# Delta-rule front of a hybrid decoder layer: another order of exponentials, bonus input and spare products

## The chip, the core and the metric

The kernel runs on one core of a Trainium2 chip. Its time is the device time in microseconds of one execution. All data are float32. The engines run their own programs side by side and meet at semaphores: TensorE (PE, with its weight loads PEld), VectorE (DVE), ScalarE (ACT), GpSimd (POOL), and SyncE (SP), whose queue issues most of the DMAs.

## The reference

Two identical layers act on 512 prompt tokens and 8 x 4 sample tokens (544 columns in the kernel). Each layer projects x to z (3592 columns), runs four mixers on groups of z, and then does an output projection, cross attention and an MLP. The change lies in the start of the fourth mixer, RWKV-7 with a delta rule:

```python
zs = z + (zprev - z) * mu                      # token shift
r, k, v, zw, za, zg = split(zs)
logw = -softplus(-(w0 + tanh(zw) @ w2)) - 0.5
decay = exp(-exp(logw))
a = sigmoid(a0 + za @ a2)
g = sigmoid(zg) @ g2
kk = k * k_k;  kk = kk / max(sqrt(sum(kk * kk)), 1e-12)
k = k * (1.0 + (a - 1.0) * k_a)
S = S * w - (S @ kk) outer (kk * a) + v outer k   # for each token
o = S @ r
bonus = sum(r * k * r_k) * v
```

## The kernel before, in words

Features lie on partitions and the 544 tokens on the free axis. z(f) is the tile of 128 features number f; T28 is z(28) and z(29), T30 is z(30) and z(31). X1, X2, X4 and X5 are scratch tiles of 2 x 544. A product by TensorE is split in two halves, of 256 and 288 columns. The first half of a product with bank number b goes to PSUM bank b, the second to bank b + 2. Each bank has a count of fillings and a count of releases, so that TensorE waits for the eviction of a bank's last content before it fills the bank again.

The projection takes w_in in slabs of 512 columns (four z tiles each), which DMAs bring into a ring with two slots. `gemm(n)` multiplies slab n, 16 products a z tile (8 of each half). The z tiles of slabs 4 to 6, and the keys and values of the memory behind them, are the list SPARE: `spare_products(pe, point, units, banks)` issues so many of its products at a place where TensorE would wait, and `spare_tiles(point)` on ScalarE evicts the halves that are complete by then. A profile shows each such product as two matmul instructions.

The order is written out by hand. On TensorE (from line 763): the products "kk" (sums of squares), tile 2 of slab 3, the wait for act_d, the products "wa" (four, two halves each) and "g2" (two, two halves each), tile 3 of slab 3, 16 spare products in banks 0 and 1 (FILL_BONUS), the wait for rk, the product "bonus", and a transpose for an output. Then the loop over five token tiles T starts: it waits for dfeat, transposes X2, X4, z(22) and z(24) ("dtok"), issues 2 spare products, waits for GpSimd's padded copies dpad, and forms the first scores ("dsc", line 815). The rest of the stage is TensorE work mixed with spare products.

On ScalarE (from line 1656): the evictions of tiles 0 to 2 of slab 3, tanh and sigmoid (act_d), the evictions of wa (sigmoid) and g2 (copy), Ln and Exp on kks (rn), the eviction of tile 3, and then, after the wait for S, three exponentials (expd 1 to 3), of X2, of X1 into T28 and of X1. The compiler puts a table load ahead of a function that the resident set lacks; `preload_act_table_set` names a set.

On VectorE (from line 1265): a scan over T28 into X1 and a subtraction into X2 (S), the wait for expd 3, two small copies into epc (the decays that the state updates read), the products of kk, the exponentials and a into X2 and X4, then X5 and rk, then r and k times their exponentials (dfeat). GpSimd copies X2 and r into padded tiles after dfeat.

Of the kernel before, what the change touches and what calls it, by code (L numbers as in the profile page):

```python
# [6 lines left out]
ALU = mybir.AluOpType  # L7
# [5 lines left out]
KC = D // P  # L13
DEPTH = 2
SEQ = 512
# [23 lines left out]
LN_EXP = "natural_log_exp_and_others"  # L39
# [6 lines left out]
ZR_D, ZK_D, ZV_D, ZWA_D, ZG_D = 20, 22, 24, 26, 27  # L46
# [173 lines left out]
def build(nc, A, O, table, where):  # L220

    with ExitStack() as ctx:
# [34 lines left out]
        def z(f, n=1):  # L257
            v = big[:, f * NT:(f + n) * NT]
            return v if n == 1 else v.rearrange("p (n t) -> p n t", n=n)
# [89 lines left out]
        sig = Signals(nc, ctx, "")  # L349
        bk = Banks(sig, psum)  # L350
        for l in range(DEPTH):
# [107 lines left out]
            omka = cols(tmp, region("tmp", 2), 2)  # L459
            mcar = cols(tmp, region("tmp", 4), 4)  # L460
            carry = cols(tmp, region("tmp", 24), 2, 12)
            epc = cols(tmp, region("tmp", 32), 2, 16)
            SsT = cols(tmp, region("tmp", 1024), 2, NB, HD)

            X1 = cols(tmp, region("tmp", 2 * NT), 2, NT)
            X2 = cols(tmp, region("tmp", 2 * NT), 2, NT)
# [60 lines left out]
            def segs(v):  # L527

                if len(v.shape) == 2:
                    return v[:, SEQ:].rearrange("p (b t) -> p b t", b=NB)  # L530
                return v[:, :, SEQ:].rearrange("p n (b t) -> p n b t", b=NB)
# [7 lines left out]
            def prm(name, i):  # L539
                return pc[:, ROWS[name][0] + i:ROWS[name][0] + i + 1]  # L540
# [70 lines left out]
            SPARE += [(n, None, nt, k) for n in range(7, 11) for nt in range(2) for k in range(KC)]  # L611
            HALF_DONE = {}

            FILL_BONUS = 2 * KC
            FILL_OM, FILL_X, FILL_ST, FILL_SA = 2, 2, 2, 1
            FILL_4 = 4
            FILL_D = (4, 16, 8)
# [3 lines left out]
            def spare_products(pe, point, units, banks, upto=None):  # L621

                at = HALF_DONE.get("at", 0)
                while at < len(SPARE) and (units > 0 if upto is None else at < upto):
                    n, f, half, k = SPARE[at]
                    key = ("kv", n - 7, half) if f is None else ("z", f, half)
                    if k == 0:
                        if half == 0 and (f is None or f == SLABS_IN[n][1]):
                            slab_pe(pe, n)
                        bk.begin(pe, key, banks[half])  # L630
                    bank = psum[:, bk.turn[key][0], :]
                    if f is None:
                        ins = pe.matmul(bank, memT[:, k, half * P:(half + 1) * P], wring[:, n % 2, k, :], start=(k == 0), stop=(k == KC - 1))  # L633
                    else:
                        c, i = HALVES[half][1], f - SLABS_IN[n][1]
                        ins = pe.matmul(bank[:, :c.stop - c.start], wring[:, n % 2, k, i * P:(i + 1) * P], xTv[:, k, c],  # L636
                                        start=(k == 0), stop=(k == KC - 1))
                    if k == KC - 1:
                        bk.filled(ins, key)
                    units -= 2 if f is None else 1  # L640
                    at += 1
                HALF_DONE["at"] = at
                HALF_DONE[point] = at // KC
# [77 lines left out]
            with nc.Block() as block:  # L721

                @block.tensor
                def _(pe):
                    def gemm(n, tiles=range(4)):
                        c0, f0 = SLABS_IN[n]
                        w = slab_pe(pe, n)
                        for i in tiles:
                            x_product(pe, ("z", f0 + i), (f0 + i) % 2, [w[:, k, i * P:(i + 1) * P] for k in range(KC)])
# [37 lines left out]
                    for i in range(2):  # L767
                        product(pe, ("kk", i), i, lambda k: kks[:, i, :], [const("sum64")])
                    gemm(3, (2,))
                    pe.wait_ge(sig["act_d"], sig.at("act_d", 2))  # L770
                    for i in range(4):
                        product(pe, ("wa", i), i % 2, lambda k: z(26)[:, :], [wwa[:, i, :]])
# [382 lines left out]
                def _(v):  # L1155
                    def one(ins):

                        after(v, ins, "v")
# [108 lines left out]
                        ins = v.tensor_tensor_scan(X1[:, i, :], const("keep_d"), T28[:, i, :], 0.0, ALU.mult, ALU.add)  # L1267
                    one(ins)
                    sig.up(tt(X2, X1, T28, ALU.subtract), "S")
                    v.wait_ge(sig["expd"], sig.at("expd", 3))  # L1270
                    v.tensor_copy(epc[:, :, 0:8], T28[:, :, 63:SEQ:64])
                    v.tensor_copy(epc[:, :, 8:16], segs(T28)[:, :, :, 3])
                    v.wait_ge(sig["rn"], sig.at("rn", 1))
                    one(tt(X4, kkr, kks, ALU.mult))
                    tt(X2, X4, X2, ALU.mult)
                    bk.given(v, ("wa", 3, 0))
                    bk.given(v, ("wa", 3, 1))
                    one(tt(X4, X4, T30, ALU.mult))
                    tt(X4, X4, X1, ALU.mult)
                    for i in range(2):  # L1280
                        ins = ts(T30[:, i, :], T30[:, i, :], prm("rwkv_k_a", i), omka[:, i:i + 1], ALU.mult, ALU.add)
                    one(ins)
                    one(tt(z(ZK_D, 2), z(ZK_D, 2), T30, ALU.mult))
                    for i in range(2):
                        ins = stt(X5[:, i, :], z(ZR_D + i), prm("rwkv_r_k", i), z(ZK_D + i), ALU.mult, ALU.mult)
                    sig.up(ins, "rk")
                    v.wait_ge(sig["rk"], sig.at("rk", 1))
                    tt(z(ZR_D, 2), z(ZR_D, 2), T28, ALU.mult)
                    sig.up(tt(z(ZK_D, 2), z(ZK_D, 2), X1, ALU.mult), "dfeat")
# [289 lines left out]
                def _(s):  # L1579
# [7 lines left out]
                    def z_tiles(n, tiles=range(4)):  # L1587

                        for i in tiles:
                            for half, c in HALVES:  # L1590
                                z_half(SLABS_IN[n][1] + i, half, c)
# [19 lines left out]
                    def spare_tiles(point):  # L1611

                        while spare_read[0] < HALF_DONE[point]:
                            n, f, half, _ = SPARE[KC * spare_read[0]]
                            if f is None:
                                kv_half(n, half)
                            else:
                                z_half(f, half, HALVES[half][1])
                            spare_read[0] += 1
# [37 lines left out]
                    s.wait_ge(sig["zs"], sig.at("zs", 2))  # L1657
                    sig.up(act(z(26)[0:64, :], z(26)[0:64, :], ACT.Tanh), "act_d")
                    sig.up(act(z(27), z(27), ACT.Sigmoid), "act_d")
                    for i in range(4):  # L1660
                        both(("wa", i), z(28 + i), ACT.Sigmoid, bias=prm(("rwkv_w0", "rwkv_a0")[i // 2], i % 2))
                    for i in range(2):
                        both(("g2", i), z(26 + i), ACT.Copy)

                    s.wait_ge(sig["ss"], sig.at("ss", 1))
                    after(s, act(kks, kks, ACT.Ln, scale=1048576.0), "s")
                    sig.up(act(kks, kks, ACT.Exp, scale=-0.5, bias=const("eps")[:, 2:3]), "rn")
                    z_tiles(3, (3,))
                    s.wait_ge(sig["S"], sig.at("S", 1))
                    sig.up(act(X2, X2, ACT.Exp, scale=-RW_C), "expd")  # L1670
                    sig.up(act(T28, X1, ACT.Exp, scale=-RW_C), "expd")
                    s.wait_ge(sig["expd"], sig.at("expd", 2))
                    sig.up(act(X1, X1, ACT.Exp, scale=RW_C), "expd")
                    spare_tiles("bonus")

                    for T in range(5):
# [1156 lines left out]
```

## Time and profile before

| quantity | value |
|---|---|
| median of 3 runs | 2476.25 us (2476.14 to 2477.13) |
| the profiled execution | 2476.93 us, of it the span 2475.0 us |
| TensorE matmul busy | 2363.3 us, 95% |
| VectorE, ScalarE busy | 41%, 19% |
| mean granted TensorE clock | 0.972 |

The time lies 1.93 us above the span. The front that the change touches runs once in each layer: from 155 to 193 us of the span, and again 1219 us later. A timeline lists instructions in order of start, merged where they follow each other; a number in brackets is the idle time of the engine before them, with what ended it.

### The profile page before, as it was taken

To read this page: it belongs to the slowest core of one execution; us is meant where nothing else is said; L and a number is where in the kernel's file an instruction comes from. 1 tells how busy PE (TensorE), PEld (TensorE's weight loads), DVE (VectorE), ACT (ScalarE), POOL (GpSimd) and SP (SyncE) were. 2 spreads that over 40 slices of the span, in tenths; PEclk is the share of its full clock that TensorE was granted. 3 is DMA by queue.
4 is the path that set the end of the run, shared out by engine and by line. 5 is a ranking of instruction groups with operands and counts; after the bars stand their busy time and mean duration, and the time that the engine had idled before them with its cause. 6 is when DMAs were issued, how large, how long until landed. Compare 5 with 4: busy or idle time off the path is not lost. (4 is left out here: it accounts for less than half of the span.)

```text
span 2475.0 us, 31491 instructions
## 1 busy us (share of the span) xinstructions
PE 2363.3 (95%) x13278; PEld 1725.5 (70%) x13278; DVE 1009.3 (41%) x1851; ACT 458.6 (19%) x965; POOL 111.1 (4%) x208
## 2 busy tenths in 40 slices
PE   7989998979999999999999899989799999999997
PEld 5867774544884788888887677655458748888886
DVE  3243224553043644566132422436331336446742
ACT  2341122010130222100023321220111312220000
POOL 0001100100000000000001011001000000000000
PEclk9999999979999999999999999989799999999998
DMA  7110003143342222232231111023432341132220
GB/s 266 42 68 19 19 35 91 47 130 120 138 171 103 85 100 71 71 100 68 68 122 68 35 37 35 24 72 98 162 136 102 120 151 54 68 102 68 90 81 36
DMA packets 137675, 215.04 MB, mean 87 GB/s; under 512 B 35528, under 2 KB 69632, under 8 KB 137408
## 3 DMA queue, kind: packets, MB, share of 16 engines
q1 hardware_dynamic: 135232, 208.84, 24.8%
q10 hardware_dynamic: 2304, 4.20, 0.5%
q8 instruction: 106, 1.74, 0.3%
q14 instruction: 33, 0.27, 0.0%
HBM read 198.43 MB, written 14.58 MB: 86 GB/s over the span
## 5 line engine op out<-in xcount | busy, mean ns | idle before, releaser
L589 PE MATMUL psum<-xT,ring 128*128 128x256 f32 (+1 forms) x1536 | 358.4, 395 | 3.2 <-ACT xT L320 1.6
L589 PEld LDWEIGHTS psum<-xT,ring 128*128 128x128 f32 x1536 | 292.3, 191 | 64.7 <-issue 3.2
L636 PE MATMUL psum<-xT,ring 128*128 128x256 f32 (+1 forms) x768 | 221.9, 415 | 0.1
L2100 PE MATMUL psum<-tmp 128*128 128x272 f32 x768 | 181.4, 393 | 0.0
L2100 PEld LDWEIGHTS psum<-tmp 128*128 128x128 f32 x768 | 145.8, 190 | 30.8 <-issue 0.8
L636 PEld LDWEIGHTS psum<-xT,ring 128*128 128x128 f32 x768 | 133.6, 191 | 41.0 <-issue 15.2
L633 PE MATMUL psum<-ring,ext 128*128 128x512 f32 x256 | 121.5, 616 | 4.5 <-ACT ext L1604 4.5
L2201 PE MATMUL psum<-big,ring 128*128 128x256 f32 (+1 forms) x512 | 118.5, 393 | 0.4 <-DMA ring<-in_w_down 0.3
L2511 PE MATMUL psum<-ring,big 128*128 128x512 f32 x256 | 113.1, 595 | 0.0
L2010 PE MATMUL psum<-ring,big 128*128 128x512 f32 x256 | 111.6, 594 | 0.0
L2201 PEld LDWEIGHTS psum<-big,ring 128*128 128x128 f32 x512 | 97.0, 190 | 20.7 <-DMA ring<-in_w_down 1.0
L2100 PE MATMUL psum<-xT,ring 128*128 128x272 f32 x448 | 107.2, 392 | 0.0
L1597 ACT ACTIVATE big<-psum 128x256 f32<-128x256 f32 (+1 forms) x112 | 44.4, 396 | 312.1 <-PE psum L589 191.9
L2100 PEld LDWEIGHTS psum<-xT,ring 128*128 128x128 f32 x448 | 85.0, 190 | 17.4
L2151 PE MATMUL psum<-big,ring 128*128 128x272 f32 x384 | 91.6, 392 | 0.0
L633 PEld LDWEIGHTS psum<-ring,ext 128*128 128x128 f32 x256 | 48.7, 199 | 60.4 <-issue 56.1
L2010 PEld LDWEIGHTS psum<-ring,big 128*128 128x128 f32 x256 | 48.0, 190 | 60.8 <-issue 60.8
L2511 PEld LDWEIGHTS psum<-ring,big 128*128 128x128 f32 x256 | 47.4, 190 | 56.9 <-issue 56.9
L2046 DVE SCALAR_TENSOR_TENSOR xtok<-xtok,psum 128x512 f32<-128x512 f32 (+1 forms) x40 | 27.3, 682 | 140.1 <-PE psum L2010 86.5
L2151 PEld LDWEIGHTS psum<-big,ring 128*128 128x128 f32 x384 | 72.6, 190 | 14.7
L2151 PE MATMUL psum<-xT,tmp 128*128 128x272 f32 x288 | 68.6, 392 | 0.0
L2151 PE MATMUL psum<-tmp 128*128 128x272 f32 x288 | 68.0, 392 | 0.0
(476 smaller groups left out, 3281.6 us busy)
## 6 DMA issues: line engine op xcount, KB each, us to landing
ring<-in_w_down SPq DMA_DIRECT2D x16, 2048.0 KB, 8.1
ring<-in_w_in SPq DMA_DIRECT2D x14, 2048.0 KB, 8.3
ring<-in_w_up SPq DMA_DIRECT2D x14, 2048.0 KB, 7.7
big<-in_cache_mem_k SPq DMA_DIRECT2D x16, 1024.0 KB, 5.0
ring<-in_xa_wk SPq DMA_DIRECT2D x4, 2048.0 KB, 7.9
ring<-in_xa_wv SPq DMA_DIRECT2D x4, 2048.0 KB, 10.3
ring<-in_w_out SPq DMA_DIRECT2D x4, 2048.0 KB, 9.3
tmp<-in_cache_mem_v SPq DMA_DIRECT2D x8, 1024.0 KB, 10.0
```

The source lines that it names most:

```text
L589: ins = pe.matmul(ps[:m, :w], lhsT_list[k], rhs(k)[:, c], start=(k == 0), stop=(k == n - 1))
L633: ins = pe.matmul(bank, memT[:, k, half * P:(half + 1) * P], wring[:, n % 2, k, :], start=(k == 0), stop=(k == KC - 1))
L636: ins = pe.matmul(bank[:, :c.stop - c.start], wring[:, n % 2, k, i * P:(i + 1) * P], xTv[:, k, c], start=(k == 0), stop=(k == KC - 1))
L1597: bk.give(act(z(f)[:, c], ps[:, 0:c.stop - c.start], fn, scale=scale), ("z", f, half))
L2010: ins = pe.matmul(ps[:n, :], left[k][:, t0:t0 + n], w[half][:, k, :], start=(k == 0), stop=(k == KC - 1))
L2046: bk.give(v.scalar_tensor_tensor(x, x, ALPHA, ps[:n, :], ALU.mult, ALU.add), key)
L2100: ins = pe.matmul(ps[:, :HT], left[:, k, :], right[:, k, :], start=(k == 0), stop=(k == KH - 1))
L2151: ins = pe.matmul(ps, left[:, k, :], right[:, k, :], start=(g == 0 and k == 0), stop=(g == 3 and k == KH - 1))
L2201: ins = pe.matmul(ps, w[r][:, k, i * P:(i + 1) * P], hT[:, 2 * KC * r + k, c], start=(r == half and k == 0), stop=(r != half and k == 2 * ...
L2511: ins = pe.matmul(ps, aT[:, k, t0:t0 + n], w[:, k, :], start=(k == 0), stop=(k == KC - 1))
```

## The change

The exponentials of the front move ahead of the eviction of z tile 3, with one named table set loaded ahead of the Ln. VectorE makes the bonus input (rk) right after S. The factor made from k_a goes to X5 instead of over T30, and a in T30 stays as it is for the product into X4. The single wait for expd 3 becomes one for expd 1 and one for expd 3 further on. Of the 16 spare products ahead of the bonus, 8 (the first half of z tile 4) move ahead of the wait for act_d, into bank 3, with their eviction ahead of those of wa. The other 8 stay, in bank 1.

```diff
-            FILL_BONUS = 2 * KC
+            FILL_BONUS = KC
@@ tensor
                     gemm(3, (2,))
+                    spare_products(pe, "wa", KC, (3, 0))
                     pe.wait_ge(sig["act_d"], sig.at("act_d", 2))
@@ vector
                     sig.up(tt(X2, X1, T28, ALU.subtract), "S")
-                    v.wait_ge(sig["expd"], sig.at("expd", 3))
-                    v.tensor_copy(epc[:, :, 0:8], T28[:, :, 63:SEQ:64])
-                    v.tensor_copy(epc[:, :, 8:16], segs(T28)[:, :, :, 3])
-                    v.wait_ge(sig["rn"], sig.at("rn", 1))
-                    one(tt(X4, kkr, kks, ALU.mult))
-                    tt(X2, X4, X2, ALU.mult)
                     bk.given(v, ("wa", 3, 0))
                     bk.given(v, ("wa", 3, 1))
-                    one(tt(X4, X4, T30, ALU.mult))
-                    tt(X4, X4, X1, ALU.mult)
                     for i in range(2):
-                        ins = ts(T30[:, i, :], T30[:, i, :], prm("rwkv_k_a", i), omka[:, i:i + 1], ALU.mult, ALU.add)
+                        ins = ts(X5[:, i, :], T30[:, i, :], prm("rwkv_k_a", i), omka[:, i:i + 1], ALU.mult, ALU.add)
                     one(ins)
-                    one(tt(z(ZK_D, 2), z(ZK_D, 2), T30, ALU.mult))
+                    one(tt(z(ZK_D, 2), z(ZK_D, 2), X5, ALU.mult))
                     for i in range(2):
                         ins = stt(X5[:, i, :], z(ZR_D + i), prm("rwkv_r_k", i), z(ZK_D + i), ALU.mult, ALU.mult)
                     sig.up(ins, "rk")
+                    v.wait_ge(sig["rn"], sig.at("rn", 1))
+                    one(tt(X4, kkr, kks, ALU.mult))
+                    v.wait_ge(sig["expd"], sig.at("expd", 1))
+                    one(tt(X2, X4, X2, ALU.mult))
+                    one(tt(X4, X4, T30, ALU.mult))
+                    v.wait_ge(sig["expd"], sig.at("expd", 3))
+                    tt(X4, X4, X1, ALU.mult)
+                    v.tensor_copy(epc[:, :, 0:8], T28[:, :, 63:SEQ:64])
+                    v.tensor_copy(epc[:, :, 8:16], segs(T28)[:, :, :, 3])
@@ scalar
                     sig.up(act(z(27), z(27), ACT.Sigmoid), "act_d")
+                    spare_tiles("wa")
...
+                    s.preload_act_table_set(LN_EXP)
                     s.wait_ge(sig["ss"], sig.at("ss", 1))
                     after(s, act(kks, kks, ACT.Ln, scale=1048576.0), "s")
                     sig.up(act(kks, kks, ACT.Exp, scale=-0.5, bias=const("eps")[:, 2:3]), "rn")
-                    z_tiles(3, (3,))
                     s.wait_ge(sig["S"], sig.at("S", 1))
                     sig.up(act(X2, X2, ACT.Exp, scale=-RW_C), "expd")
                     sig.up(act(T28, X1, ACT.Exp, scale=-RW_C), "expd")
                     s.wait_ge(sig["expd"], sig.at("expd", 2))
                     sig.up(act(X1, X1, ACT.Exp, scale=RW_C), "expd")
+                    z_tiles(3, (3,))
                     spare_tiles("bonus")
```

## Rows read from the trace of the kernel before

**Rows 1.** The page, part 1: busy time, share of the span, instructions of TensorE.

```profile
PE 2363.3 (95%) x13278; PEld 1725.5 (70%) x13278; DVE 1009.3 (41%) x1851; ACT 458.6 (19%) x965; POOL 111.1 (4%) x208
```

**Rows 2.** The waits of TensorE, whole span: total, times, longest.

```profile
PE psum L589 <- DVE tmp L1285: 10.9, 2, 5.5
...
PE psum L589 <- ACT big L1659: 6.0, 2, 3.0
...
PE psum L2201 <- DMA ring<-in_w_down: 0.3, 1, 0.3
```

**Rows 3.** Timeline of TensorE, layer 0: start, length, line, shapes, count, idle before.

```profile
147.81 7.50 PE L589 MATMUL psum<-xT,ring 128*128 128x256 f32 x32
158.31 7.45 PE L589 MATMUL psum<-big,tmp 128*128 128x256 f32 x24 [3.01 <-ACT big L1659]
166.20 7.57 PE L589 MATMUL psum<-xT,ring 128*128 128x256 f32 x32 [0.43 <-ACT big L1624]
...
186.54 4.00 PE L589 MATMUL psum<-tmp,con 128*128 128x256 f32 x8 [5.44 <-DVE tmp L1285]
...
190.54 1.06 PE L802 MATMUL psum<-con,tmp 128*128 128x128 f32 x4
...
193.34 1.08 PE L815 MATMUL psum<-xtok,tmp 128*64 128x256 f32 x8
```

**Rows 4.** Windows: length, busy time of each engine, granted clock, DMA.

```profile
158.31:166.20 7.89, 7.46 (x25) 5.64 (x25) 3.27 (x3) 5.20 (x12) 0.00 (x0) 0.78 0.00 0
166.20:181.10 14.90, 14.90 (x64) 12.04 (x64) 4.18 (x6) 9.25 (x11) 0.00 (x0) 1.00 0.42 140
186.54:193.34 6.80, 6.80 (x21) 5.37 (x22) 4.45 (x7) 1.20 (x2) 1.59 (x4) 0.56 0.01 2
```

**Rows 5.** Timeline of ScalarE, same stretch.

```profile
162.19 2.58 ACT L1624 ACTIVATE big<-psum,tmp 128x288 f32<-128x288 f32 x5 [0.31 <-PE psum L589]
164.81 1.69 ACT L1624 ACTIVATE big<-psum 128x256 f32<-128x256 f32 x4
166.51 1.28 ACT L1666 ACT_TABLE_LOAD   x1
...
168.93 1.28 ACT L1667 ACT_TABLE_LOAD   x1
...
176.24 1.11 ACT L1673 ACTIVATE tmp<-tmp 128x1088 f32<-128x1088 f32 x1
```

**Rows 6.** Timeline of VectorE, same stretch.

```profile
162.90 2.48 DVE L1267 TENSOR_TENSOR_SCAN tmp<-con,big 128x544 f32<-128x544 f32 x2 [10.99 <-ACT big L1624]
...
177.56 1.29 DVE L1274 TENSOR_TENSOR tmp<-xtok 128x1088 f32<-128x1088 f32 x1
...
182.62 1.03 DVE L1281 TENSOR_SCALAR big<-big,tmp 128x544 f32<-128x544 f32 x2
183.68 1.29 DVE L1283 TENSOR_TENSOR big<-big 128x1088 f32<-128x1088 f32 x1
185.01 1.48 DVE L1285 SCALAR_TENSOR_TENSOR tmp<-big,tmp 128x544 f32<-128x544 f32 x2
...
187.73 1.28 DVE L1289 TENSOR_TENSOR big<-big,tmp 128x1088 f32<-128x1088 f32 x1
```

**Rows 7.** Timeline of GpSimd, same stretch.

```profile
190.56 0.40 POOL L1810 COPY xtok<-big 64x256 f32<-64x256 f32 x1
```

**Rows 8.** Timeline of TensorE at the second token tile.

```profile
269.42 0.66 PE L802 MATMUL psum<-con,tmp 128*128 128x128 f32 x4
...
271.30 1.08 PE L815 MATMUL psum<-xtok,tmp 128*64 128x256 f32 x8
```

**Rows 9.** Timeline of ScalarE, end of the stage: a named set loaded ahead.

```profile
403.15 1.28 ACT L1746 ACT_TABLE_LOAD   x1 [0.47 <-ACT ext L1604]
...
416.23 1.11 ACT L1743 ACTIVATE big<-big 128x1088 f32<-128x1088 f32 x1
```

**Rows 10.** DMA view, 124 to 134 us, 40 slices of 0.25 us: rate of each.

```profile
GB/s 41 16 57 164 262 360 401 385 336 319 344 377 410 418 410 410 418 393 401 385 401 426 401 385 246 123 82 16 0 0 0 0 0 0 0 0 0 0 0 0
```

## The prediction

> **What bounds the kernel now.** I read four views, in this order. The page's first part: TensorE is busy for 95% of the span [rows 1]. All its work stays, so only its idle time and its slowed time can be won or lost. The waits of TensorE come next. In the whole span only a few stand out, and two lie in the front: for the act_d sigmoid, 6.0 us over the two layers, and for the bonus input, 10.9 us over the two layers [rows 2]. Then the timelines of the front of layer 0. TensorE idles 3.01 us ahead of wa, 0.43 ahead of z tile 3, and 5.44 ahead of the bonus [rows 3]. Last the windows, for the clock. After the idle 3.01 us the granted clock is 0.78 on average up to 166.20, after 5.44 it is 0.56 up to 193.34, and between them, with the gap of 0.43 just before, it is 1.00 [rows 4]. These are mixtures of the two levels, 1.2 and 2.4 GHz. So each long gap costs its own length and then slow work behind it. In layer 1 the same waits come back with the same lengths, so I work out layer 0 and double it.
>
> **What a layer can give back.** The idle time is 3.01 + 0.43 + 5.44 = 8.9 us. The slow work: the 24 instructions of wa and g2 take 7.5 us, and a z tile's 32 take 7.50 at the full clock [rows 3], 0.234 each, so they would take 5.6: 1.8 lost. The 8 of the bonus and a transpose take 4.00 from 186.54 to 190.54, where 9 would take 2.0: 2.0 lost. From the first dtok transpose to the first dsc product the same work takes 2.80 here [rows 3] and 1.88 at the next token tile [rows 8]: 0.9 lost. Together 13.6 us a layer. Now I lay out the changed order to see what it keeps of that.
>
> **The first half of z tile 4 moved ahead of act_d.** TensorE comes there at 155.31 (147.81 + 7.50). Eight products of 256 columns are 256/544 of a tile, 3.5 us, 3.6 with the tail: to 158.9. It fills the gap that ends at 158.31, so wa begins 0.6 later than before, but at the full clock. Two waits come with it. The slab must be in the ring: its transfer runs from about 124 to 131 us [rows 10], more than 24 us early. Bank 3 must be free: its last user, the second half of kk, came before tile 2 of slab 3, which itself took 7.5 us. Behind the new eviction on ScalarE stand the wa evictions, but it starts at 158.9, takes what the 256-column evictions of g2 take (1.69 for four, 0.42 each [rows 5]), and the first wa product is only full at 159.4. It is free. Its cover is TensorE's own first wa product of 0.5 us; without it the 0.4 would be on the path. SP's queue sees the same order: slab 5 waits for tile 3 of slab 3, and its issue moves with that. If some 13 us of other work behind it vanish, it still has the rest of slab 4 in front of it, 56 products, over 25 us of TensorE.
>
> **wa, g2 and S.** At the full clock ScalarE limits this piece: five wa evictions in 2.58 us, 0.52 each [rows 5]. Four are done by 161.5, eight by 163.6, g2 at 165.3. VectorE's scan waited for the fourth and began at 162.90 [rows 6]. Now it begins at 161.7, and with 2.48 for the scans and 1.29 for the subtraction S is there at 165.5. TensorE finishes g2 at about 164.5 and waits for bank 1: tile 3 began 1.39 after the first g2 eviction (164.81 to 166.20), so now at 165.0. That is 0.5 idle, like the 0.43 before, which was followed by a clock of 1.00. Tile 3 ends at 172.4.
>
> **The bonus input made without the exponentials.** After S VectorE does only the k_a step (1.03), the product (1.29) and the r_k step (1.48): from 182.62 to 186.5 in the old order, 3.9 us. So rk comes at 169.4 instead of 186.5. TensorE is then in tile 3 and the 5.44 us wait is gone with 7 us to spare. What is late next is ScalarE and dfeat.
>
> **The table and the exponentials.** Before, Ln and Exp each have a load of 1.28 [rows 5]. The named set at the end of the stage serves a Ln and then an Exp with no load between them; one load stands at 403.15 and the Exp at 416.23 is reached without another [rows 9]. So one load remains: from 165.3 the load to 166.6, Ln to 167.8, Exp to 169.0 (rn, before at 171.4). S is long there, and three exponentials of 1.11 (less a little overlap) end at 172.1 instead of 177.35.
>
> A page sees the table otherwise. The Trainium skill, ScalarE: Activation LUTs, section "What ACT_TABLE_LOAD costs", gives 1283 ns for the load and about 1380 ns more for a drain, 2.66 us a switch. The trace shows the 1.28, with Ln starting within 0.03 us of the load's end. By the page's figure, an estimate, the exponentials would end 1.4 later and the forecast lose about 2.8 us over both layers; the row decides for me.
>
> **The eviction of z tile 3 behind them.** Both halves are late now, and bank 1 is wanted by the spare half that stays ahead of the bonus. The first half of tile 3 is evicted from 172.1 to 172.5, and TensorE is done with tile 3 at 172.4: idle 0.1. The second half follows at once. If the exponentials ended later, each microsecond would fall on TensorE: this is the tightest place of the new order. The spare half of 288 columns takes 3.9, to 176.4, and the bonus 1.9, to 178.3. A transpose of 0.1 follows, and dtok could begin at 178.4 instead of 190.54.
>
> **dfeat.** VectorE starts the kk product at 169.4 (rn at 169.0 is there). With a step of 1.32 (a product and the wait for its write) three products reach 173.4; expd 1 (170.0) and expd 3 (172.1) are there in time. The product with X1 (1.25), two copies (0.2) and the last two products (2.5) give dfeat at 177.3, instead of 189.0 [rows 6]. GpSimd then takes its four copies, which ended at 190.96, 1.95 after dfeat [rows 7]: at 179.3. TensorE begins dtok at 178.4 and reaches dsc at 180.3. Both are 1.0 us ahead of need. In VectorE's queue the bonus evictions stand behind dfeat and end at 178.8, before dsc wants it. The two copies into epc cost 0.2 and are hidden by that 1.0; the added waits for writes cost 0.04 each.
>
> **The sum.** dsc at 180.3 instead of 193.34 is 13.05 us: the 13.6 to be had less 0.55 of new idle time. Two layers give 26.1. All waits of TensorE behind it hang on work that moves along; only one transfer row lies behind the front, 0.3 us [rows 2]. So the profiled execution's 2476.93 becomes 2450.8; it lies 0.7 above the median, so the median becomes 2450.2.
>
> **The rivals.**
> *The clock does not come back* (0.12). The gap of 0.5 at 164.5, or one left in a place I misjudge, still lets it fall once in the front. For it: it fell after each of the two long gaps. Against it: 1.00 after 0.43. One slow piece costs what one costs here, 1.8 to 2.9 a layer, so 2450.2 + 3.6 to 5.8: 2454 to 2456.
> *The table is not kept* (0.08). If each of Ln and Exp is still given its load, that part of the change does not do what it says: the exponentials end 1.3 later, 173.4, and the spare half starts 1.2 to 1.3 late. dfeat moves by less. It is 2.5 us over both layers, 2453, and with another load for the following exponentials and a slow piece up to 2461.
> *Hidden elsewhere* (0.04). If the next stage were held by something that does not move, a transfer above all, nothing would come: 2476. Against it speak the 0.3 us of TensorE's waits on w_down [rows 2].
> *Slower* (0.03). The moved half makes wa wait for slab 4. It decides once the slab lands more than 13 us after 155.3, at 168; a landing at 175 would give 7 us a layer of loss, 2490. The transfer is over at 131.
>
> **Chances and range.** The forecast's own case has 0.73, from 2447 to 2455. Its upper end has the page's drain, or a step of 1 to 2 us at the tight place in each layer; its lower end has all 13.6 and a slow piece less behind later gaps of the stage (about 1 us a layer). The two next cases reach to 2461. I give 2446 to 2460. About 0.2%, 5 us, is what a measurement of this kernel can tell from no change. Faster by more: 0.73 + 0.12 + 0.08 = 0.93; within: 0.04; slower: 0.03.
>
> **What would show it.** In the timeline of the changed kernel: 16 instructions of spare products in the old gap at 155.3; wa at 158.9 and tile 3 at 165.0; a clock of 1.00 from 155 to 181; one table load and rk at 169.4; tile 3's evictions after 172.1; bonus at 176.4 without idle time, dtok at 178.4, dsc at 180.3. The forecast is wrong if the spare half starts well after 172.5, if dfeat is later than 178.4, if a slow piece stands anywhere in the front, or if the waits behind 193 us grow.

## The result, and the profile after

| | before | changed |
|---|---|---|
| median in the runs side by side | 2476.25 us (5 runs) | 2452.03 us (5 runs, 2449.74 to 2452.35) |
| ratio of the times | | 0.99, 95% interval 0.9889 to 0.9912 |
| profiled execution, span | 2476.93, 2475.0 us | 2451.32, 2449.4 us |

The change makes the kernel 24.2 us faster. The forecast was 26.1, so 2450.2. The page of the changed kernel gives the span and the busy times (compare [rows 1]):

```profile
span 2449.4 us, 31491 instructions
...
PE 2356.6 (96%) x13278; PEld 1719.7 (70%) x13278; DVE 1009.8 (41%) x1851; ACT 455.5 (19%) x963; POOL 110.6 (5%) x208
```

TensorE's busy time is 6.7 us less for the same 13278 matmuls, because fewer of them ran at the lower clock. The waits of TensorE (total, times, longest) no longer hold the two of [rows 2]. The gap ahead of tile 3 is what is left of the front. The wait at L981 far behind the front stayed, and so did the small one for a transfer:

```profile
PE psum L981 <- DVE tmp L1409: 7.1, 2, 3.6
...
PE psum L589 <- ACT big L1626: 1.1, 2, 0.6
...
PE psum L2205 <- DMA ring<-in_w_down: 0.2, 1, 0.2
```

The timeline of TensorE through the front of layer 0, which answers to [rows 3], follows. Everything lies 1.42 us earlier from the start, since tile 2 begins at 146.39 instead of 147.81. The whole of it is there within the first 56 us, ahead of every changed instruction; 1.1 us of it is the wait for the kernel's first transfer, 16.7 us in the trace before and 15.6 in this one. So it is no part of the change, and I add it where I compare with the forecast's times.

```profile
146.39 7.50 PE L589 MATMUL psum<-xT,ring 128*128 128x256 f32 x32
153.72 3.62 PE L636 MATMUL psum<-xT,ring 128*128 128x256 f32 x16
157.18 5.66 PE L589 MATMUL psum<-big,tmp 128*128 128x256 f32 x24
163.39 7.57 PE L589 MATMUL psum<-xT,ring 128*128 128x256 f32 x32 [0.55 <-ACT big L1626]
170.81 4.15 PE L636 MATMUL psum<-xT,ring 128*128 128x288 f32 x16
174.80 2.00 PE L589 MATMUL psum<-tmp,con 128*128 128x256 f32 x8
...
176.75 0.60 PE L803 MATMUL psum<-con,tmp 128*128 128x128 f32 x4
...
178.58 1.08 PE L816 MATMUL psum<-xtok,tmp 128*64 128x256 f32 x8
```

Where two gaps of 3.01 and 5.44 us stood, one row follows the other. The spare half (153.72) fills the first. wa takes 5.66 instead of 7.45, the bonus 2.00 instead of 4.00, and the four dtok transposes 0.60 instead of 1.06. The timeline of ScalarE (compare [rows 5]):

```profile
157.38 0.38 ACT L1599 ACTIVATE big<-psum 128x256 f32<-128x256 f32 x1 [0.54 <-PE psum L636]
...
163.71 1.28 ACT L1668 ACT_TABLE_LOAD   x1
165.00 1.11 ACT L1670 ACTIVATE xtok<-xtok 128x1088 f32<-128x1088 f32 x1
...
169.38 1.11 ACT L1676 ACTIVATE tmp<-tmp 128x1088 f32<-128x1088 f32 x1
170.39 0.37 ACT L1599 ACTIVATE big<-psum 128x256 f32<-128x256 f32 x1
```

There is one table load, with Ln beginning at its end, and the exponentials end at 170.5, with tile 3's eviction behind them. VectorE (compare [rows 6]): the scan, the r_k step that gives rk at 167.6, the kk product that follows at once, and the last product that ends in dfeat at 175.4, 13.6 us earlier than before and 1.3 us before TensorE wants it.

```profile
160.09 2.48 DVE L1268 TENSOR_TENSOR_SCAN tmp<-con,big 128x544 f32<-128x544 f32 x2 [9.60 <-ACT big L1626]
...
166.20 1.48 DVE L1278 SCALAR_TENSOR_TENSOR tmp<-big,tmp 128x544 f32<-128x544 f32 x2
167.60 1.29 DVE L1281 TENSOR_TENSOR tmp<-xtok 128x1088 f32<-128x1088 f32 x1
...
174.15 1.28 DVE L1291 TENSOR_TENSOR big<-big,tmp 128x1088 f32<-128x1088 f32 x1
```

The windows (length, busy time of PE, PEld, DVE, ACT and POOL with counts, granted clock, DMA) show the clock at 1.00 throughout, where [rows 4] had 0.78 and 0.56:

```profile
155.30:159.00 3.70, 3.70 (x18) 3.17 (x17) 0.00 (x0) 3.00 (x6) 0.00 (x0) 1.00 0.00 0
159.00:165.00 6.00, 5.45 (x25) 4.29 (x24) 4.84 (x6) 5.68 (x11) 0.00 (x0) 1.00 0.00 0
165.00:172.50 7.50, 7.50 (x33) 5.91 (x32) 7.36 (x7) 6.11 (x7) 0.00 (x0) 1.00 0.06 7
172.50:178.00 5.50, 5.50 (x30) 4.57 (x29) 4.98 (x10) 1.03 (x3) 1.58 (x4) 1.00 1.00 360
```

### The profile page after: what moved, and what is told of

It reads as the page before. It is cut to its first block and busy times, and to the rows that moved or that the text cites. A ratio compares the mean times of both kernels' runs of the same rounds, so it can differ in the third digit from the quotient of the medians.

```text
span 2449.4 us, 31491 instructions
## 1 busy us (share of the span) xinstructions
PE 2356.6 (96%) x13278; PEld 1719.7 (70%) x13278; DVE 1009.8 (41%) x1851; ACT 455.5 (19%) x963; POOL 110.6 (5%) x208
## 5 line engine op out<-in xcount | busy, mean ns | idle before, releaser
L1599 ACT ACTIVATE big<-psum 128x256 f32<-128x256 f32 (+1 forms) x112 | 44.3, 396 | 312.6 <-PE psum L589 187.9
L2104 PEld LDWEIGHTS psum<-xT,ring 128*128 128x128 f32 x448 | 85.0, 190 | 17.4
```

Source lines behind the costliest of these rows:

```text
L1599: bk.give(act(z(f)[:, c], ps[:, 0:c.stop - c.start], fn, scale=scale), ("z", f, half))
L2104: ins = pe.matmul(ps[:, :HT], left[:, k, :], right[:, k, :], start=(k == 0), stop=(k == KH - 1))
```

## The experiments

To compare kernels I cut the span at four starts that each trace has: z tile 2 of slab 3, the first dsc product, the transposes of the sample states (L980 in the kernel before, some 240 us in), and the first product of the output projection. Front is the time from the first to the second, loop from the second to the third, rest from the third to the fourth, in us, layer 0 / layer 1. "Between" goes from the output projection of layer 0 to tile 2 of slab 3 in layer 1, "behind" from the output projection of layer 1 to the end of the span. These are differences of starts in the timelines, of one profiled execution a kernel; medians are those of the timed runs.

| kernel | median | front | loop | rest | between | behind |
|---|---|---|---|---|---|---|
| before | 2476.25 | 45.5 / 45.3 | 204.1 / 204.1 | 155.4 / 157.3 | 814.0 | 701.6 |
| changed | 2452.03 | 32.2 / 32.2 | 205.7 / 205.7 | 155.5 / 155.5 | 814.7 | 701.4 |
| e1_half_only | 2475.81 | 43.1 / 43.1 | 205.7 / 205.7 | 155.5 / 155.6 | 814.2 | 704.1 |
| e2_order_only | 2460.74 | 36.8 / 36.7 | 205.6 / 205.7 | 155.5 / 157.3 | 814.1 | 701.3 |
| e3_no_set | 2455.89 | 33.5 / 33.5 | 205.6 / 205.7 | 155.5 / 157.3 | 814.4 | 701.7 |
| e4_tile_first | 2455.56 | 34.9 / 34.9 | 207.2 / 204.2 | 155.5 / 155.4 | 814.7 | 703.9 |
| e5_input_late | 2465.09 | 39.8 / 39.3 | 205.7 / 205.8 | 155.5 / 155.6 | 811.7 | 703.9 |
| e6_no_set_bank0 | 2455.52 | 32.9 / 32.9 | 205.7 / 205.7 | 155.5 / 155.5 | 814.2 | 704.3 |
| e7_half_before_tile | 2447.92 | 31.3 / 31.3 | 207.2 / 204.2 | 155.6 / 155.5 | 811.5 | 704.1 |
| e8_more_fill | 2434.77 | 32.2 / 32.2 | 205.7 / 205.7 | 146.3 / 148.1 | 814.2 | 701.2 |
| e9_both | 2430.95 | 31.3 / 31.3 | 205.6 / 204.1 | 147.9 / 147.9 | 814.2 | 701.1 |
| e10_mixed_small | 2443.81 | 32.2 / 32.2 | 206.1 / 206.2 | 152.3 / 152.2 | 811.3 | 704.0 |
| e11_all | 2446.63 | 31.3 / 31.3 | 206.1 / 206.1 | 150.3 / 153.1 | 814.3 | 704.3 |
| e12_mixed_same | 2436.26 | 31.3 / 31.3 | 206.2 / 208.0 | 146.5 / 147.9 | 814.5 | 704.1 |

e8, e9, e11 and e12 have some 3.6 us of spare products in the loop where a wait was, and e10 and e11 have 3.4 us of them set among other matmuls of the loop. The kernel before, run beside these, had medians from 2475.01 to 2476.82.

**e1_half_only: the moved half alone.**

```diff
 (against the kernel before)
-            FILL_BONUS = 2 * KC
+            FILL_BONUS = KC
                     gemm(3, (2,))
+                    spare_products(pe, "wa", KC, (3, 0))
...
                     sig.up(act(z(27), z(27), ACT.Sigmoid), "act_d")
+                    spare_tiles("wa")
```

> The kernel before with only the spare half of z tile 4 moved ahead of act_d. My theory: the wait ahead of wa (3.0 us) goes and wa runs at the full clock, but TensorE has 8 spare products fewer ahead of the bonus and rk comes only some 1.2 us earlier, because it hangs on the three exponentials and the old order on VectorE. The wait ahead of the bonus grows from 5.4 to about 9 us. dtok gains 1.2 us a layer: 2474 us. Rival, parts that add up: the filled gap gives its 3.0 and 1.8 us in each layer by itself: 2466.5 us.

2475.81 us against 2475.01 of the kernel before beside it, ratio 1.0002 (0.9993 to 1.0012): no difference. TensorE in layer 0, as it ends the spare half, waits for the bonus, and begins dtok:

```profile
171.48 4.04 PE L636 MATMUL psum<-xT,ring 128*128 128x288 f32 x16
184.41 3.93 PE L589 MATMUL psum<-tmp,con 128*128 128x256 f32 x8 [8.89 <-DVE tmp L1286]
...
188.29 0.60 PE L803 MATMUL psum<-con,tmp 128*128 128x128 f32 x4
```

The wait for rk is 8.89 us, as expected. The wait ahead of wa went into it. The front is 2.2 to 2.5 us shorter, more than the 1.2 that I gave it, because the clock is back by dtok this time (0.60 for the four transposes). So filled by itself, the first gap mostly makes the second longer, and the parts do not add up: the fronts of both layers gain 4.6 us here, 17.4 in e2_order_only, and 26.4 together. Why nothing at all is left in the time, the trace shows in pieces that the edit does not touch: the loops are 1.6 us longer in each layer and the piece behind is 2.6 longer, against 1.7 less in the rest of layer 1.

**e2_order_only: the new order alone.**

```diff
 (against the changed kernel)
-            FILL_BONUS = KC
+            FILL_BONUS = 2 * KC
                     gemm(3, (2,))
-                    spare_products(pe, "wa", KC, (3, 0))
...
-                    spare_tiles("wa")
```

> The changed kernel with all 16 spare products back ahead of the bonus, so only the new order on ScalarE and VectorE and the single table load. My theory: the wait for rk (5.4 us) and the slow work behind it (2.9 us) go, the gap ahead of wa stays with its slow work: 8.3 us a layer, 2459.6 us. Rival, idle time alone counts and the clock does not: 10.9 us in all, 2465.4. If the parts added up, this gain and that of the half alone would make the whole 24.2 us; I expect them to make about 19.

2460.74 us (0.9939, 0.9924 to 0.9954). The gap ahead of wa and its slow work are there, and the bonus follows without any:

```profile
157.95 7.31 PE L589 MATMUL psum<-big,tmp 128*128 128x256 f32 x24 [3.01 <-ACT big L1660]
...
180.43 2.00 PE L589 MATMUL psum<-tmp,con 128*128 128x256 f32 x8
```

The front gained 8.8 and 8.6 us a layer, where 8.3 was expected and idle time alone would give 5.4. The clock's part is real. In the times the two halves of the change give 0 and some 14 us by themselves and 24 together.

**e3_no_set: the table load back.**

```diff
 (against the changed kernel)
-                    s.preload_act_table_set(LN_EXP)
```

> The changed kernel without the named table set, so that Ln and Exp have a load each again. My theory: the eviction of z tile 3 stands behind the exponentials and TensorE's spare half waits for its bank, so the 1.3 us of a load fall on TensorE in full: an idle 1.2 to 1.4 us ahead of the spare half in each layer, 2454.5 us, or up to 2 us more if the clock falls behind that gap. Rival: the exponentials have slack, nothing changes, 2452. By the drain that a page of the Trainium skill gives (ScalarE: Activation LUTs, What ACT_TABLE_LOAD costs) the load would cost 2.66 us, an estimate of 2457.

2455.89 us, 3.9 more than the changed kernel. TensorE waits ahead of the spare half, by the eviction of tile 3 (L1599):

```profile
172.73 4.15 PE L636 MATMUL psum<-xT,ring 128*128 128x288 f32 x16 [1.13 <-ACT big L1599]
```

The front is 1.3 us longer in each layer: one load of 1.28, in full, as forecast, and with no drain beside it: in this trace the second load begins 0.02 us after the end of the Ln, and the Exp 0.02 us after the load's. The Trainium skill's 2.66 us for a switch (ScalarE: Activation LUTs, What ACT_TABLE_LOAD costs) would have made it 2.7 us a layer, an estimate; the measurement is 1.3. The times show 1.3 us more than the two fronts; in the trace the rest of layer 1 is 1.8 us longer, 157.3 instead of 155.5, far from the change.

**e4_tile_first: tile 3 evicted ahead of the exponentials.**

```diff
 (against the changed kernel)
+                    z_tiles(3, (3,))
                     s.wait_ge(sig["S"], sig.at("S", 1))
...
                     sig.up(act(X1, X1, ACT.Exp, scale=RW_C), "expd")
-                    z_tiles(3, (3,))
```

> The changed kernel with z tile 3 evicted ahead of the exponentials again. My theory: the second half of the tile is only full at 172.4 in the forecast's frame, the exponentials end 4 us later, VectorE waits for the first of them at 170.8 until about 173.9, and dfeat comes at 180.4 instead of 177.3. TensorE waits about 2.1 us for dfeat ahead of dtok, in each layer, and the clock may fall behind that gap for another 1 to 2 us: 2456 to 2460 us. The bonus input is not touched and TensorE does not wait for it. Rival: dfeat has slack enough and nothing changes, 2452.

2455.56 us, 3.5 more. The wait is for dfeat (the last product of VectorE, L1291), ahead of dtok, and a second small one follows ahead of dsc:

```profile
177.70 0.66 PE L803 MATMUL psum<-con,tmp 128*128 128x128 f32 x4 [2.28 <-DVE big L1291]
...
179.89 1.08 PE L816 MATMUL psum<-xtok,tmp 128*64 128x256 f32 x8 [0.23 <-DVE tmp L1295]
```

The front is 2.7 us longer. The 2.28 agrees with the 2.1 forecast. The clock did not fall behind it inside the front (1.00 from 176 to 184 us). By the medians only 3.5 us are lost where two fronts make 5.4; the profiled execution was the slowest of the four, 6.1 us above that of the changed kernel. And the loops of the two layers differ by 3.0 us, 207.2 and 204.2, at the same program.

**e5_input_late: VectorE in the old order.**

```diff
 (against the changed kernel; the block up to rk as before)
+                    v.wait_ge(sig["expd"], sig.at("expd", 3))
+                    v.tensor_copy(epc[:, :, 0:8], T28[:, :, 63:SEQ:64])
+                    v.tensor_copy(epc[:, :, 8:16], segs(T28)[:, :, :, 3])
+                    v.wait_ge(sig["rn"], sig.at("rn", 1))
+                    one(tt(X4, kkr, kks, ALU.mult))
+                    tt(X2, X4, X2, ALU.mult)
...
```

> The changed kernel with VectorE's part in the old order: the wait for all three exponentials first, the bonus input last. My theory: rk comes 9.1 us after the third exponential (172.1 in the forecast's frame), at 181.2, and TensorE is ready for the bonus at 176.4: a wait of 4.8 us and some 3 us of slow work behind it in each layer, 7.7 us, so 2467 us. Rival, idle time alone: 2461.6. Rival, the early exponentials are what gives the gain and the order on VectorE nothing: 2452.

2465.09 us, 13.1 more. The bonus waits 4.72 us and runs slowly again, the front is 7.6 and 7.1 us longer:

```profile
177.98 3.99 PE L589 MATMUL psum<-tmp,con 128*128 128x256 f32 x8 [4.72 <-DVE tmp L1286]
```

**e6_no_set_bank0: no set, and the spare half in another bank.**

```diff
 (against the changed kernel)
-                    s.preload_act_table_set(LN_EXP)
...
-                    spare_products(pe, "bonus", FILL_BONUS, (0, 1))
+                    spare_products(pe, "bonus", FILL_BONUS, (0, 0))
```

> The changed kernel without the named table set, as in an earlier run, and with the second spare half in bank 0 instead of bank 1. Bank 0 is free once g2 is evicted, so the spare half no longer waits for the eviction of z tile 3. My theory (the table's price is paid through that bank): the 1.3 us a layer come back almost whole, because dfeat is then at 178.3 against TensorE's 178.4: 2452, at most 2453.5. Rival (the price is paid elsewhere, in rn and dfeat): it stays as slow as without the set in bank 1.

2455.52 us, so by the times my number was missed. In the trace the wait ahead of the spare half is gone, as it should be if the price is paid through bank 1. But the bonus's own first half goes into bank 0 as well and now waits for the eviction of the spare half, which I had overlooked:

```profile
176.35 2.08 PE L589 MATMUL psum<-tmp,con 128*128 128x256 f32 x8 [0.59 <-ACT big L1599]
```

The front is 0.7 us longer than changed instead of 1.3. The theory of the bank holds, the repair was only half of one. The two fronts make 1.4 of the 3.5 us by which the kernel is slower; the piece behind is 2.8 us longer, where the program is the same.

**e7_half_before_tile: the second half moved too.**

```diff
 (against the changed kernel)
-                    gemm(3, (3,))
-                    spare_products(pe, "bonus", FILL_BONUS, (0, 1))
+                    spare_products(pe, "bonus", FILL_BONUS, (0, 0))
+                    gemm(3, (3,))
...
-                    z_tiles(3, (3,))
                     spare_tiles("bonus")
+                    z_tiles(3, (3,))
```

> The changed kernel with the second spare half moved ahead of z tile 3, into bank 0, and its eviction ahead of that of tile 3. My theory: it fills the 0.55 us that TensorE waits for bank 1 behind g2 and removes the dependence on the exponentials; dtok comes 0.6 us earlier in each layer, 1.2 us in all, too little for the times to tell (2450.8 against 2452.0) but seen in the timeline: no idle time ahead of tile 3, dsc 0.55 earlier. Rival: dtok then waits for dfeat or dsc for the padded copies and nothing moves.

2447.92 us, 4.1 less than changed. The front is 0.9 us shorter in each layer (0.6 forecast) and has no gap:

```profile
156.03 5.66 PE L589 MATMUL psum<-big,tmp 128*128 128x256 f32 x24
161.53 4.04 PE L636 MATMUL psum<-xT,ring 128*128 128x288 f32 x16
165.41 7.50 PE L589 MATMUL psum<-xT,ring 128*128 128x256 f32 x32
```

The remaining 2.3 us are not the front's. In the trace the piece between the layers is 3.2 us shorter, the start 1.1, and the piece behind 2.6 longer.

**e8_more_fill: a gap elsewhere, filled the same way.**

```diff
 (against the changed kernel)
-                            spare_products(pe, ("Sss",), FILL_4, (0, 1))
+                            spare_products(pe, ("Sss",), FILL_4 + 8, (0, 1))
```

> The changed kernel with 8 more units (4 products of the memory's keys and values) at the wait for the sample states behind the delta rule, where TensorE still idles 3.6 us in each layer. My theory, that a gap of this length costs itself and slow work behind it: the 3.6 us and about 1.7 us of slow work go, and the products are missing later only where they stood in front of nothing: up to 5 us a layer, 2442. Rival: the slab of the third product is not there yet, or the units are missing at a later wait, and TensorE waits just as long there: 2452.

2434.77 us, 17.3 less than changed, where I had expected at most 10. Two gaps of the changed kernel in layer 0:

```profile
384.28 1.09 PE L981 MATMUL psum<-con,tmp 128*128 128x128 f32 x8 [3.56 <-DVE tmp L1409]
...
399.92 2.10 PE L589 MATMUL psum<-big,con 128*128 128x256 f32 x8 [2.21 <-ACT big L1742]
```

With the four added products (eight instructions) the row ahead of L981 ends as L981 begins, and the second gap is gone too:

```profile
379.51 5.42 PE L633 MATMUL psum<-ring,ext 128*128 128x512 f32 x12
385.07 1.09 PE L981 MATMUL psum<-con,tmp 128*128 128x128 f32 x8
```

The loop is as long as before, with products in place of the wait, and the rest is 9.2 and 7.4 us shorter: some 3.6 are those products, 2.2 the second gap, and the other 1.6 to 3.4 slow work. I had counted one gap only. The rest can be shorter by those products because they were only moved: they stand in the loop now.

**e9_both: both edits.** The diff is that of e7_half_before_tile and e8_more_fill.

> The two edits that were fastest by themselves together: the second spare half ahead of z tile 3, and 8 more units at the wait for the sample states. The stretches should add, since they lie 200 us apart: the front 31.3 us (0.9 less than changed) and the stretch behind the sample states 8 to 9 us less than changed. Changed 2452.0, the fill alone 2434.8, less 1.8: 2433 us, with 1 to 3 us either way for where the clock falls later. Rival, the clock's own pieces swallow it: 2435 to 2437.

2430.95 us, ratio 0.9819 to the kernel before (0.9805 to 0.9834), 21 us less than the changed kernel: the two add up, and of all versions run this is the fastest.

**e10_mixed_small: the clock inside the loop.** The changed kernel's windows of 2 us near the end of the loop of layer 0 (length, busy times, clock):

```profile
344.00:346.00 2.00, 2.00 (x60) 1.68 (x58) 1.45 (x3) 0.00 (x0) 0.00 (x0) 1.00 0.04 8
346.00:348.00 2.00, 2.00 (x59) 1.92 (x56) 0.00 (x0) 1.57 (x3) 0.00 (x0) 0.95 0.00 0
348.00:350.00 2.00, 2.00 (x28) 1.89 (x27) 0.00 (x0) 1.97 (x3) 0.00 (x0) 0.50 0.00 0
```

TensorE is busy without a break and its clock falls to 0.50 all the same, where the products that read the sample states stand, 128 matmuls of four columns in 64 rows each:

```profile
344.32 2.03 PE L922 MATMUL psum<-xtok,tmp 64*64 64x4 f32 x64
...
346.65 2.66 PE L931 MATMUL psum<-xtok,tmp 64*64 64x4 f32 x64
...
351.21 3.79 PE L636 MATMUL psum<-xT,ring 128*128 128x288 f32 x8
```

In the front 16 instructions of spare products of 288 columns take 4.15 us; here eight take 3.79. The same place in the kernel before:

```profile
361.39 2.13 PE L930 MATMUL psum<-xtok,tmp 64*64 64x4 f32 x64
...
365.43 2.68 PE L636 MATMUL psum<-xT,ring 128*128 128x288 f32 x8
```

There the clock falls as well, but a little later, and it is back after some 3.5 us; in the changed kernel it stays at 0.50 for some 7 us. From the start of the first 64 to the end of the eight instructions it is 9.0 us before and 10.7 in the changed kernel, with the same work. This is where the loop gave back 1.6 us a layer. The experiment sets spare products among them:

```diff
 (against the changed kernel, in the branch of the last token tile)
+                                if pr == 0:
+                                    spare_products(pe, ("KSmid", 0), 2, (0, 1))
                             bk.filled(ins, ("KS",))
+                            spare_products(pe, ("KSmid", 1), 2, (0, 1))
...
+                                if pr == 0:
+                                    spare_products(pe, ("KSmid", 2), 2, (0, 1))
                             sig.up(ins, "Dstates")
```

> The changed kernel with 6 more spare units set among the 128 matmuls of four columns that read the sample states at the last token tile (2 in the middle of the first 64, 2 behind them, 2 in the middle of the other 64). In the changed kernel the clock falls inside this run although TensorE has no idle time, and stays at half for some 7 us. Theory A, the clock falls because the four-column matmuls keep the array little busy: with full-sized products between them it stays at 1.00, which gives back 3 to 3.5 us a layer; the wait of 3.6 us behind may shrink too, as the 2.8 us of added products lie in front of it and are missing only in the rest behind: 2440 to 2446 us. Theory B, the fall comes from elsewhere (a fixed budget or a moment): the clock still falls there and only the wait behind may shrink: 2450 us.

2443.81 us, 8.2 less than changed, with one of the four runs at 2449.75. The second 64 matmuls now take 1.10 for each 32, the product between them is fast, and the clock is 1.00:

```profile
347.69 1.10 PE L934 MATMUL psum<-xtok,tmp 64*64 64x4 f32 x32
348.72 1.18 PE L636 MATMUL psum<-xT,ring 128*128 128x288 f32 x4
349.84 1.10 PE L934 MATMUL psum<-xtok,tmp 64*64 64x4 f32 x32
```

```profile
349.00:351.00 2.00, 2.00 (x37) 1.55 (x37) 0.00 (x0) 1.97 (x3) 0.00 (x0) 1.00 0.00 0
```

The three pieces of added products take 3.4 us, and the loop is only 0.4 longer, so 3.0 us shorter for the same work. The wait at the sample states did not shrink; it is 4.07 us. Loops and rests together are 5.6 us shorter in the two layers. The piece between them is 3.4 shorter and the piece behind 2.6 longer, neither of which the edit touches.

**e11_all: all three edits.** The diff is that of e9_both and e10_mixed_small.

> All three edits together: second spare half ahead of z tile 3, 8 more units at the sample states, 6 units among the four-column matmuls. If theory A of the mixed matmuls holds, 6 to 7 us less than the two edits without it: 2427 us; if the clock falls there anyway, 2433.

2446.63 us (2440.79 to 2451.33): a miss, 16 us slower than e9_both. The clock stays up in the loops as in e10. But of the 13.1 us that the span is longer than that of e9_both, 7.5 are in the rest of the two layers, 2.4 in the loops and 3.2 behind the rest of layer 1. In the rest a wait is new:

```profile
PE psum L1055 <- DVE xtok L1459: 3.4, 2, 1.7
```

In e9_both ten instructions of spare products, 4.46 us, stand at that place; here none is left. Within 2 us behind the wait the clock falls. In the rests of the two layers it is at half for some 45 and 52 us, in e9_both for 39 and 38. The piece behind is 704.3 instead of 701.1, which other kernels show too; the last section tells what differs in it.

**e12_mixed_same: the same number of units, four of them in other places.**

```diff
 (against e9_both)
+                                if pr == 0:
+                                    spare_products(pe, ("KSmid", 0), 2, (0, 1))
                             bk.filled(ins, ("KS",))
...
+                                if pr == 0:
+                                    spare_products(pe, ("KSmid", 2), 2, (0, 1))
                             sig.up(ins, "Dstates")
                             swap(0)
-                            spare_products(pe, ("KS",), FILL_4, (0, 1))
+                            spare_products(pe, ("KS",), 0, (0, 1))
```

> The kernel of the two fastest edits (second spare half ahead of z tile 3, 8 more units at the sample states; 2430.95 us) with the 4 units that stood behind the four-column matmuls of the last token tile moved among them, 2 into the middle of each 64. The number of spare products at every later place is the same, unlike in the runs with 6 more units. If the clock falls there because the four-column matmuls keep the array little busy, it now stays at 1.00 and 1.5 to 3.5 us a layer come back: 2424 to 2428 us. If 16 us of later stages suffered in the run of all three edits for another reason than the missing units, it is again near 2440. If the place of the products does not matter: 2431.

2436.26 us, 5.3 more than e9_both: a miss, and none of the three forecasts (2424 to 2428, 2431, 2440) fits. The loops are 4.5 us longer in the trace, the piece behind 3.0, the rest of layer 0 1.4 shorter. With 4 units instead of 6 the clock fell, and it fell earlier, so that a spare product itself ran slowly (2.14 us for four instructions instead of 1.24):

```profile
342.46 1.24 PE L636 MATMUL psum<-xT,ring 128*128 128x288 f32 x4
...
346.05 2.14 PE L636 MATMUL psum<-xT,ring 128*128 128x288 f32 x4
348.12 1.87 PE L933 MATMUL psum<-xtok,tmp 64*64 64x4 f32 x32
```

So spare products among the four-column ones kept the clock up with six units, in both layers, and did not with four. Whether their number decides, or the place of the missing two (between the two groups of 64), was not tried.

## Why the prediction was right

**The front.** Every step came as written. In the forecast's frame, with the shift of 1.42 added: wa at 158.6 (158.9 forecast), tile 3 at 164.8 (165.0), the scan at 161.5 (161.7), rk at 169.0 (169.4), the third exponential's end at 171.9 (172.1), the spare half at 172.2 (172.5), the bonus at 176.2 (176.4), dfeat at 176.9 (177.3), dtok at 178.2 (178.4), dsc at 180.0 (180.3). The gain is 13.3 and 13.1 us a layer where 13.05 was the sum. The differences all begin with wa's 0.3 us, and two readings share it. The spare half starts 7.33 us after tile 2, not 7.50, because rows that follow each other overlap a little and the forecast added the row's length. And it takes 3.46 us from its start to that of wa, not 3.6.

**What it is made of.** e2 shows the clock's share: 8.7 us of front for 5.4 us of gap. e1 shows that the moved half is worth 2.2 to 2.5 us of front while rk is late, and the whole change has 4.5 to 4.6 more of it than e2's order alone, e5 that the bonus input made early is worth 7.1 to 7.6 us a layer, e4 that the order of exponentials and tile eviction is worth 2.7, e3 that the table load is worth 1.3. e3 and e6 show that the last is paid at the eviction of tile 3, the place that the forecast called the tightest, with a step of 1.3 for a load of 1.28.

**The rivals.** The clock came back and stayed at 1.00 through the front, so the first rival fell there. The table was kept; the drain that the Trainium skill gives is not in the trace, and e3 prices the load without it. The slab was in the ring, and no transfer took the gain: the one transfer wait behind the front is 0.2 us.

**What was mis-sized.** 1.9 us between 26.1 and 24.2, 0.5 between the spans (25.6). The step "all waits of TensorE behind it hang on work that moves along" is right, but the slow pieces do not simply move along. The loop went from 204.1 to 205.7 us in each layer, 3.2 us given back, because the clock stays at half for some 7 us there instead of 3.5; the rest of layer 1 gained 1.8; the long piece between the layers went from 814.0 to 814.7; the start gave 1.4 that has nothing to do with the change. 26.4 - 3.2 + 1.8 - 0.8 + 1.4 is 25.6. So the fronts came by the mechanism that was forecast, and that the total lies so near is partly luck: the other pieces moved by 0.8 to 3.2 us and happened to cancel almost. In e1, e4, e5, e6 and e7 the piece behind is 2.3 to 2.7 us longer than in the kernel before, with the same program; here it kept its length. The forecast had allowed about 1 us a layer for a slow piece less, and nothing for one more, which is what came.

## What to carry to other kernels

Where the busiest engine waits at two places in a row, ask what the second wait hangs on before the first is filled: the filler alone gave nothing in the time (2.2 to 2.5 us a layer in the front), the earlier input alone 14 us, both 24. Price a long gap of TensorE with the slow work behind it: behind the gaps of 3.0 us and more it was half as much again, and filling two gaps of 5.8 us together gave 7 to 9 a layer. The shorter ones have no fixed price: 2.28 us in e4 was followed by no slow work in the front, 1.7 us in e11 was. And compare spans cut at the same instructions, for a change at one place can give or take a few microseconds at places that it does not touch.

## What the runs showed of the hardware

**The clock falls inside busy TensorE.** In every kernel but e10 and e11 the granted clock goes to 0.50 during or just behind 128 matmuls of four columns, in both layers, with no idle time in the rows. It stays there for some 3.5 us, some 7, or some 10. The work in it pays by its kind. Full-sized products take about twice their time (eight instructions 3.79 us, 1.94 at 1.00). The four-column ones pay nearly as much, 3.58 us for 64 instead of 2.03, as here in e9_both:

```profile
345.21 3.58 PE L931 MATMUL psum<-xtok,tmp 64*64 64x4 f32 x64
```

**The same program, another fall.** In the kernels from before to e9 the loop takes 204.1, 205.7 or 207.2 us, in steps of 1.6, and the length goes with how long the clock stays at half at those matmuls: 3.5 us in the loops of 204.1 and 204.2, 7 in those of 205.6 to 205.8, 10 in those of 207.2. In e4 and e7 the two layers of one execution differ by 3.0 us. The rest takes 155.4 to 155.6 or 157.3. The pieces between and behind have two lengths as well, 811.3 to 811.7 or 814.0 to 814.7, and 701.1 to 701.7 or 703.9 to 704.3. What differs lies at two places. In the long form the clock stays at half longer at the start of the output projection, and it falls again some 70 us further on, behind a wait of 2.70 us, where eight instructions (L2410) take 1.97 us. In the short form it does not fall there, and they take 1.15. I did not find what decides which form comes. The length of the front alone does not: in e4 and e7 it is the same in both layers, and the loops differ. With one profile for each kernel it is also not known whether one kernel keeps its form from one execution to the next. So a forecast for this kernel can be off by some 2 to 3 us for each such piece.

**What is left.** In the changed kernel the clock is at half for some 42 us of the rest of each layer, far more than in the loop. No run here tried to change that.
